# Stage 3 of a hybrid layer: router with its weights stationary on four column groups, narrow query-state products, sums of squares on two column groups

## The reference

```python
o_inter = jnp.einsum('bhnck,bhnkv->bhncv', q_dec, s_prev)      # added to o_intra
o = _rmsnorm(o, gla_norm_g) * jax.nn.silu(r)                   # over the 128 values of a head
u = jax.nn.silu(_layernorm(u, conv_ln_g, conv_ln_b))           # over 512 channels
out = jnp.einsum('btc,cd->btd', jnp.concatenate([o, u], axis=-1), w_out)
x = x + gt1 * out
h = _rmsnorm(x, norm_ffn_g) * (1.0 + sc2) + sh2
logits = jnp.einsum('btd,de->bte', h, w_router)                # 16 experts
aff = jax.nn.softmax(logits, axis=-1)                          # then top-k tokens of each expert
```

## Time and profile before

| | us |
|---|---|
| median of 3 runs | 2609.25 (2609.11 to 2611.84) |
| span of the profiled execution | 2605.0 |
| PE busy in it | 2388.8 |
| stage 3, from its first product (L1772) to its last logits | about 807.7 to 1218.8 |

### The profile page before, as it was taken

The page is one execution under the profiler, slowest core; times in us unless marked ns, Lnnn a source line. Parts: engine busy times, 40 slices in busy tenths (PEclk is TensorE's granted clock), DMA queues, the critical chain, the costliest instruction groups (busy, mean ns, idle before and its releaser), DMA issues.

```text
span 2605.0 us, 41287 instructions
## 1 busy us (share of the span) xinstructions
PE 2388.8 (92%) x15500; PEld 2138.2 (82%) x15500; DVE 1653.4 (63%) x2793; ACT 1189.2 (46%) x1916; POOL 735.0 (28%) x671
## 2 busy tenths in 40 slices
PE   5879999999995899996569999999999999999994
PEld 1868878787894577875169999999999999999994
DVE  1797969689597554523836656666665666666575
ACT  2646354453422333331145555445555545555563
POOL 1000000000000130110033445554445555444451
PEclk9989999999996899997579999999999999999997
DMA  7885575746536556524255667776667776666885
GB/s 242 322 305 193 175 252 182 262 164 227 189 127 207 166 161 143 166 96 128 70 151 185 180 199 199 199 212 191 188 182 205 199 206 196 188 187 196 280 253 193
DMA packets 287555, 505.73 MB, mean 194 GB/s; under 512 B 32094, under 2 KB 230587, under 8 KB 271578
## 3 DMA queue, kind: packets, MB, share of 16 engines
q1 hardware_dynamic: 248042, 377.93, 44.2%
q0 software_dynamic: 39408, 126.38, 18.7%
HBM read 405.73 MB, written 98.53 MB: 194 GB/s over the span
## 4 chain that ended last, share of the span: by engine, by line
PE 57%; DVE 5%; DMA 3%; ACT 2%; issue 1%; POOL 1%; SPq 0%; DVEq 0%; ACTq 0%; POOLq 0%
PE bank L1519 17%; PE bank L1521 17%; PE bank L1520 17%; PE bank L1764 1%; PE bank L1832 1%; DMA work_out<-park_s 1%; DVE work_exp L2511 1%; DMA out_dram<-work_exp 1%; PE bank L1780 1%; PE bank L1821 1%; DVE work_proj L2258 1%; PE bank L1783 1%; DVE work_out L2305 1%; PE bank L1772 1%; POOL x_rows L1458 0%
## 5 line engine op out<-in xcount | busy, mean ns | idle before, releaser
L1519 PE MATMUL bank<-act_hl_exp,hl_exp 128*128 128x288 f32 x3072 | 913.6, 297 | 37.2 <-POOL act_hl_exp L1437 24.0
L1520 PE MATMUL bank<-act_hl_exp,hl_exp 128*128 128x288 f32 x3072 | 910.2, 296 | 0.0
L1521 PE MATMUL bank<-act_hl_exp,hl_exp 128*128 128x288 f32 x3072 | 908.7, 296 | 0.0
L1519 PEld LDWEIGHTS bank<-act_hl_exp,hl_exp 128*128 128x128 f32 x3072 | 579.8, 189 | 40.6 <-issue 28.9
L1521 PEld LDWEIGHTS bank<-act_hl_exp,hl_exp 128*128 128x128 f32 x3072 | 581.8, 189 | 0.0
L1520 PEld LDWEIGHTS bank<-act_hl_exp,hl_exp 128*128 128x128 f32 x3072 | 580.6, 189 | 0.0
L2629 DVE TENSOR_TENSOR hl_exp<-work_exp,hl_exp 128x1024 fp32r<-128x1024 f32 x192 | 231.7, 1227 | 228.5 <-ACT hl_exp L1126 228.5
L2629 DVE TENSOR_TENSOR hl_exp<-raw_exp,hl_exp 128x1024 fp32r<-128x1024 f32 x192 | 232.2, 1225 | 200.5 <-ACT hl_exp L1126 200.5
L2258 DVE SCALAR_TENSOR_TENSOR work_proj<-work_proj,wcv 128x392 f32<-128x392 f32 (+11 forms) x600 | 337.0, 634 | 0.0
L1126 ACT ACTIVATE hl_exp<-work_exp 128x1024 fp32r<-128x1024 f32 x192 | 199.4, 1055 | 218.5 <-PE bank L1521 213.0
L1126 ACT ACTIVATE hl_exp<-raw_exp 128x1024 fp32r<-128x1024 f32 x192 | 198.5, 1052 | 166.5 <-PE bank L1521 166.4
(11 more groups left out here) (330 smaller groups left out, 3456.0 us busy)
## 6 DMA issues: line engine op xcount, KB each, us to landing
hl_proj<-park_w POOLq DMA_DIRECT2D x80, 1024.0 KB, 5.5
raw_exp<-in_w_e_gate_dram SPq DMA_DIRECT2D x32, 1024.0 KB, 5.7
raw_exp<-in_w_e_up_dram SPq DMA_DIRECT2D x32, 1024.0 KB, 5.7
work_exp<-in_w_e_gate_dram SPq DMA_DIRECT2D x32, 1024.0 KB
work_exp<-in_w_e_up_dram SPq DMA_DIRECT2D x32, 1024.0 KB, 6.4
raw_exp<-in_w_e_down_dram SPq DMA_DIRECT2D x32, 1024.0 KB, 5.5
work_exp<-in_w_e_down_dram SPq DMA_DIRECT2D x32, 1024.0 KB, 5.5
park_w<-hl_proj SPq DMA_DIRECT2D x10, 2048.0 KB, 11.8
```

What stands on the lines that cost most here:

```text
L1519: pe.matmul(out, lh, rh, start=first, stop=False)
L1520: pe.matmul(out, lh, rl, start=False, stop=False)
L1521: return pe.matmul(out, ll, rh, start=False, stop=last_)
```

## The change

- `router(g)` swaps its operands. Eight products with 32 columns of `wrA` stationary (16 of this chunk, and 16 of the next, whose result isn't used) and 128 tokens moving, for chunk k into partitions 32*(k%4) to 32*(k%4)+31 of the bank: four column groups, two products each. The result is 16 experts x 128 tokens in four partial sums. DVE's new `logit_rows(g)` copies the 128x128 floats to `lgT`; a new product `router_sum(g)` has `lgT` stationary and `selg` (16 columns, which pick the four groups) moving, and gives 128 tokens x 16 experts in bank 4. `logit(g)` reads them there.
- `row_T(g)` writes bank 4, so it now waits for `logit(g-1)`. `out_half` now waits for `logit_rows` where it waited for `logit`.
- `inter` makes every product in two halves of 64 stationary columns, into partitions 0 to 63 and 64 to 127.
- `sums` puts the convolution's products into partitions 0 to 31 and the heads' into 32 to 63, each with 32 stationary columns, one of each in turn. What works on the result takes 64 partitions instead of 5, and `spread` multiplies over 128 partitions instead of 64.

The core of the diff:

```diff
                     for cc in range(NC3[m]):
-                        last = pe.matmul(psum[7 - h % 2][:, 64 * cc:64 * cc + 64], S3[:, cc + 1, 128 * h:128 * h + 128],
-                                         part("q", m, h)[:, 64 * cc:64 * cc + 64], start=True, stop=True)
-                    last.then_inc(r_in, 1)
+                        for v in (0, 64):
+                            ins = pe.matmul(psum[7 - h % 2][v:v + 64, 64 * cc:64 * cc + 64],
+                                            S3[:, cc + 1, 128 * h + v:128 * h + v + 64],
+                                            part("q", m, h)[:, 64 * cc:64 * cc + 64], start=True, stop=True)
...
             def sums(m):
                 pe.wait_ge(r_o1, 4 * m + 3)
-                for ct in range(4):
-                    pe.wait_ge(r_csq, 4 * m + ct + 1)
-                    pe.matmul(psum[7][0:5, 0:T3[m]], selc[:, 4, :], part("sq", m, ct), start=(ct == 0), stop=False)
                 for h in range(H):
+                    pe.wait_ge(r_csq, 4 * m + h + 1)
+                    conv = pe.matmul(psum[7][0:32, 0:T3[m]], sel_conv, part("sq", m, h), start=(h == 0), stop=(h == 3))
...
                     pe.wait_ge(r_sq, 4 * m + h + 1)
-                    last = pe.matmul(psum[7][0:5, 0:T3[m]], selc[:, h, :], part("q", m, h), start=False, stop=(h == 3))
-                last.then_inc(r_st, 1)
+                    head = pe.matmul(psum[7][32:64, 0:T3[m]], sel_head[h], part("q", m, h), start=(h == 0), stop=(h == 3))
...
             def row_T(g):
                 upto(pe, r_xn, g + 1)
                 if g >= 1:
                     pe.wait_ge(r_ev, 2 * g)
+                    pe.wait_ge(r_lg, g)
...
                 for k in range(KC):
-                    last = pe.matmul(psum[logit_bank(g)][:, 0:NE], h2T[:, g % 2, k, :], wrA[:, c, k, :], start=(k == 0),
-                                     stop=(k == KC - 1))
-                last.then_inc(r_ro, 1)
+                    o, i = 32 * (k % 4), NE * (KC * c + k)
+                    ins = pe.matmul(psum[logit_bank(g)][o:o + 32, 0:128], W3["wrA"][:, i:i + 32], h2T[:, g % 2, k, :],
+                                    start=(k < 4), stop=(k >= 4))
+                    if k >= 4:
+                        ins.then_inc(r_ro, 1)
+
+            def router_sum(g):
+                upto(pe, r_lt, g + 1)
+                pe.matmul(psum[4][:, 0:NE], lgT[:, g % 2, :], W3["selg"], start=True, stop=True).then_inc(r_co.sem, 1)
...
+            def logit_rows(g):
+                dve.wait_ge(r_ro, 4 * g + 4)
+                dve.tensor_copy(lgT[:, g % 2, :], psum[logit_bank(g)][:, 0:128]).then_inc(r_lt.sem, 1)
+
             def logit(g):
                 m = M_OF[g]
-                dve.wait_ge(r_ro, g + 1)
-                dve.tensor_tensor(logits[:, ROW3[m] // 128 + g - G3[m], :], psum[logit_bank(g)][:, 0:NE],
+                upto(dve, r_co, g + 1)
+                dve.tensor_tensor(logits[:, ROW3[m] // 128 + g - G3[m], :], psum[4][:, 0:NE],
                                   brow[:, 0 if m == 0 else 1, :], ALU.add).then_inc(r_lg, 1)
```

More of the change, by code:

```diff
@@ L1351, in _ @@
             pool.wait_ge(r_sel, 2)
-            for h in range(5):
-                pool.memset(selc[:, h, h:h + 1], 1.0 if h < H else DV / 512.0).then_inc(r_sel, 1)
+            pool.memset(sel_head[0][:, 0:1], 1.0).then_inc(r_sel, 1)
+            pool.memset(sel_conv[:, 0:1], DV / 512.0).then_inc(r_sel, 1)
             def routing_constants():
@@ L1813, in out_half @@
                                  wo_hl[:, 1, k, 512 * q:512 * q + 512], k == 0, k == KC - 1)
-                last.then_inc(r_T.sem, 1)
+                if k1 == KC:
+                    last.then_inc(r_T.sem, 1)
             def row_T(g):
@@ L1863, in stage3 @@
                     router(g0 - 2)
-                out_half(g0, 1)
+                    out_half(g0, 1, 0, 4)
+                    router_sum(g0 - 2)
+                    out_half(g0, 1, 4, KC)
+                else:
+                    out_half(g0, 1)
                 if m > 0:
@@ L1872, in stage3 @@
                     inter(prep, (0, 1))
-                out_half(g0 + 1, 0)
+                    if m > 0:
+                        router_sum(g0 - 1)
+                    out_half(g0 + 1, 0)
+                else:
+                    out_half(g0 + 1, 0, 0, 4)
+                    router_sum(g0 - 1)
+                    out_half(g0 + 1, 0, 4, KC)
                 if prep:
@@ L1880, in stage3 @@
                     sums(prep)
-                if NT3[m] == 2:
-                    spread(prep)
-                    return
-                out_half(g0 + 2, 0)
+                    router_sum(g0)
+                    if NT3[m] == 2:
+                        spread(prep)
+                        return
+                    out_half(g0 + 2, 0)
+                else:
+                    out_half(g0 + 2, 0, 0, 4)
+                    router_sum(g0)
+                    out_half(g0 + 2, 0, 4, KC)
                 row_T(g0 + 1)
@@ L1889, in stage3 @@
                 router(g0 + 1)
-                out_half(g0 + 3, 0)
+                out_half(g0 + 3, 0, 0, 4)
+                router_sum(g0 + 1)
+                out_half(g0 + 3, 0, 4, KC)
                 if not prep:
@@ L2437, in stage3 @@
                 if NT3[m] == 2:
+                    logit_rows(g0)
                     logit(g0)
@@ L2442, in stage3 @@
                 residual(g0 + 1)
+                logit_rows(g0)
+                inverse(g0 + 1)
                 logit(g0)
-                inverse(g0 + 1)
                 if prep:
@@ L2448, in stage3 @@
                 residual(g0 + 2)
+                logit_rows(g0 + 1)
+                inverse(g0 + 2)
                 logit(g0 + 1)
-                inverse(g0 + 2)
                 if not prep:
+                    logit_rows(g0 + 2)
                     logit(g0 + 2)
@@ L2473, in _ @@
             inverse(NTILE - 1)
+            logit_rows(NTILE - 1)
             logit(NTILE - 1)
```

81 lines of the change are left out of this document (50 added, 31 removed).

## The result

The changed kernel takes 2573.11 us (median of 4 runs, 2572.41 to 2579.72), the kernel before 2609.18 (4 runs, 2607.85 to 2611.84): ratio 0.9864, interval 0.985 to 0.9878, or 36.1 us less. Measured again beside other kernels it was 28.6 and 32.75 us faster. The forecast was 21 us less, and 2577 us the lower end of its range: the sign and the waits came as forecast, the size did not.

The account below looks back on a forecast made before the run. PE was taken to bound stage 3 until another engine's chain is late. Block terms of -24.5 us, changeovers +1.6 and clock +1.5 made -21.4, giving 2588 us, range 2577 to 2607.

Parts of the forecast that it names:

- the clock: Stage 3: new pauses in blocks 2 and 3 may trigger stretches at 1.2 GHz; -3 to +6 us, taken +1.5.
- the slots: Router and sums: 16 passes take 9 slots, 0.96 us for the router and 3.87 us for a block's sums.
- the changeovers: PE, entering and leaving some 32 groups of narrow products: 0 to 3.2 us, taken +1.6.
- What bounds: Stage 3: PE is busy throughout mid-block windows, so PE time spared comes off until another engine's chain is late.
- groups fully side by side: Rival: both passes of a product overlap too, router 4 or 5 slots, sums 8; 2583 us, chance 0.19.
- The path: Stage 3, block by block: prologue -4.4, block 0 -6.05, block 1 -6.75, blocks 2 and 3 -8.6, end +1.3; sum -24.5 us.
- The new waits: Blocks 2 and 3: `row_T` waits for logits, +1.6 us; second head waits for `centre`; block 4 idles about 3 us.
- Outside stage 3: Code before and after stage 3: nothing changes, 0 us.
- Loads apart: Rival: products overlap but loads don't, `inter` stays at 3.5 us a pair; 2602 us, chance 0.20.
- no overlap: Rival: column groups don't overlap and the change costs time, together +14 us; 2623 us, chance 0.16.
- doesn't do what it says: Router: passes cost more than 0.107 us because 128 columns of `h2T` move at another rate; the rest, chance 0.03.

Follow-up runs that it names:

- stores_block4: Changed kernel with the four small stores to mod_d issued in block 4 instead of block 2: 2566.61 us, ratio 0.9837 to the kernel before.
- the two repeats: The unedited changed kernel measured twice more against the kernel before: 2584.25 us (ratio 0.9884) and 2576.27 us (0.9871).
- the single parts: Kernel before with one part of the change each: only the sums 2597.33 us, only narrow query-state products 2604.48 us, only the router 2605.63 us.
- inter_only: Kernel before with only the query-state products (`inter`) in halves of 64 columns: 2604.48 us, ratio 0.996.
- router_only: Kernel before with only the router swapped, with its summing product, copy `logit_rows` and new waits: 2605.63 us, ratio 0.9963.

## Why the prediction was wrong in size and right in its path

The order of the waits was right. Three terms of the sum failed: the clock (taken +1.5, measured -8.7 net in blocks 1 to 4), the slots (9 of 16 taken, 8 and 4 measured) and the changeovers (+1.6 taken, next to nothing measured). Another 3.85 us lie outside stage 3 and are not the change's.

**What bounds.** Right. PE was spared time in the middle of blocks, and it came off until DVE's list was late, at the places named.

**Slots.** The step that failed first: "the two passes of one product use the same group and can't overlap, so the second pass of one product can run only beside the first of the next", and from it 9 slots of 16. The passes of two sums run side by side through and through, 8 slots, and the router takes 0.46 us instead of 0.96. The order of records, the only argument against the rival of groups fully side by side, says nothing on when they run. A pair of `inter` took 2.02 instead of 1.8 us. In a block at full clock this is some -0.5 for a router and -0.45 for the sums, against the forecast, and +0.2 for a pair.

**Changeovers**, taken at 1.6: next to nothing. Block 2 before and block 2 of `stores_block4` both have a clock of 1.00 and no pauses: 75.98 and 70.76, -5.2. Read group by group from the two timelines, the new wait costs +1.8 (forecast 1.6), the span from the transposes to the end of the first pair gives -1.4 (-1.75), the second pair -1.5 (-1.75), the router ahead of the sums -1.3 (-0.7), the sums -3.4 (-3.0), and the other three summing products take 0.24 each (0.4). These make -5.1, so there is nothing left for some eight changeovers. The router's 16 records take 0.46 us to the sums, which also have 32 columns, and 0.57 to the pair, which has 64: this change of the tile's width costs 0.1 us. The Trainium skill ("TensorEngine Tiling (Array Packing)", Key Properties) says that such a change of the tiling mode drains the engine; by these rows the drain, if there is one, is within that 0.1 us, and the sum of the block leaves no room for more. And where the Trainium skill has a speedup of 2.38 for three column groups ("TensorE: Matmul & The Clock Gate", Part 3), this case has 3.8 for four.

**The path**, the profiled execution against the forecast, with half of the change in time at 1.2 GHz taken out of blocks 1, 3 and 4:

| | forecast | measured | of it clock | rest |
|---|---|---|---|---|
| prologue | -4.4 | -4.45 | | -4.45 |
| block 0 | -6.05 | -6.2 | | -6.2 |
| block 1 | -6.75 | -9.7 | -5.4 | -4.3 |
| block 2 | -4.3 | -1.6 | | -5.2, and +3.6 from the stores and behind the new wait |
| block 3 | -4.3 | -8.3 | -3.4 | -4.9 |
| block 4, end | +1.3 | +0.7 | -1.4 | +2.1 |
| changeovers | +1.6 | | | 0 |
| clock | +1.5 | | | |

The -5.2 of block 2 is that of `stores_block4`, another execution; the rest is from the profile of after. The last column sums to -23.0 without the 3.6, where the forecast has -22.9 with its changeovers. That agreement is luck, errors that cancel: slots and changeovers worth some 5 us more than forecast (an estimate from the paragraphs above), block 1 and block 4 less. (Block 1's forecast counted 2.6 us at the place where the clock was low, so part of the clock's gain was in it.)

**The clock** is the term that was mis-sized most: "-3 to +6, taken +1.5", and it gave -10.2 in blocks 1, 3 and 4 of the profiled execution and some +1.5 in block 2, -8.7 in all (half of 41.1 less 23.7). In the two repeats it was half of 15.3 and of 14.2, -7.7 and -7.1. The step asked what new pauses would trigger, and they did trigger stretches, of 3.4 us. It did not ask what becomes of the stretches that were there. The earlier trace rows showed one, in a place where the change takes away most of the work; the single parts show that less work there is enough to remove it.

**The new waits.** Right in place and cause, the first a little longer than forecast: `row_T` waits for the logits (2.29 and 2.32 us, 1.5 to 2 forecast; logits forecast to end at +5.55 us from the second half of the scan, measured 5.40), the second head 0.92 (0.7), the third tile starts 2.36 us after its router (2.4), block 4 idles 2.86 (about 3).

**Not in the forecast at all:** the pauses that the small stores make in the second pair. In the profiled execution they and a stretch of the clock are the 3.6 us of block 2 (the pair takes 3.1 instead of 2.02 us, the clock 1.5, ACT comes 0.9 late behind it); the other runs show up to 9 us in block 2 (`inter_only`, 76.0 to 85.3).

**Outside stage 3** the forecast had 0, and the two executions differ by 3.85 us, which no edit explains. Together, with half of the new stretch of block 2 inside the 3.6: -23.0 - 10.2 + 3.6 - 3.85 = -33.45, against the span's -33.5.

Of the rivals, "groups run fully side by side" was the true mechanism. Its 2583 us missed by the same clock term, and it had counted the routers only: eight slots instead of nine for the sums of four blocks are another 1.7 us, 2581. Loads apart, no overlap and "doesn't do what it says" are out by the rows of the router, the sums and the pair.

## What to carry to other kernels

Small products in different column groups run fully side by side, both passes, if neighbours in program order use different groups: count rounds, not records (a round is one pass in each group), and don't count on less than about 0.03 us for a record at the full clock, the shortest seen here. When a part of the path shrinks, look in DVE's list at what used to be covered by it, and move short operations that PE waits for ahead of long ones: here that was worth 14 us of stage 3, where the largest part of the change, the sums, gave 16. When a change shortens a piece in which the clock was low, ask what becomes of that stretch: here it went from that place each time, but `inter_only` got as much back elsewhere, so give the term a range on both sides. And keep DMAs in tiny elements away from a place where PE runs many short instructions.

## What the runs showed that was not expected

- Records of two column groups start within 0.01 us of each other, for all 16 passes of the sums; 16 router passes on four groups take 0.46 us, on one group 1.77 us.
- A pair of `inter` in alternating halves takes 2.02 us, in separate halves 3.34 us. In the prologue at 1.2 GHz 32 such records take 1.97 us, 0.062 us each, at 2.4 GHz 0.032 us: this shortest time of a record goes with the clock.
- Four stores of 4 KB in 4-byte elements take a DMA share of 0.85 at 1 GB/s. Moved to block 4 they give the changed kernel 9.7 us (2576.27 to 2566.61), 3.9 of them in block 2 of the profiles, and the kernel before nothing (ratio 1.0, 0.999 to 1.001).
- A packet of the instruction queue that mostly takes 0.9 to 1.1 us took 3.6 (`before`) to 8.2 us (`router_only`) beside these stores.
- Stretches at 1.2 GHz of about 7 us start while PE is busy all of the time, inside the first pair of `inter` of before (seven of nine blocks). With the router or the pair made short there are none at that place (six blocks).
